# Near attention's first two batches moved into the last product of the values, with the PSUM banks turned round, three bias loads in one place and products of ones around a norm

## What is computed

```python
s_loc = jnp.einsum('bhrqd,bhrikd->bhrqik', qg, kg) * scale + bias      # bias gathered from rpb
s_loc = jnp.where(col_mask[:, None, :], s_loc, NEG_INF)
s_ctx = jnp.einsum('bhrqd,bhcd->bhrqc', qg, k_c) * scale
p = jax.nn.softmax(jnp.concatenate([s_loc, s_ctx], axis=-1), axis=-1)
o = einsum(p_loc, vg) + einsum(p_ctx, v_c)
x = x + g1 * (merge(o) @ odd_w_o)
x = x + g2 * conv_ffn(modulate(x, norm2_g, sh2, sc2), ...)
```

## Time and profile before

| what | us |
|---|---|
| median of 3 runs | 1559.91 (1559.86 to 1560.09) |
| the profiled execution | 1558.57 |
| its span, first to last instruction | 1556.8 |
| PE busy | 1529.9 (98%) |
| DVE busy | 1035.4 (67%) |
| ACT busy | 758.2 (49%) |
| POOL busy | 100.6 (6%) |

### The profile page before, as it was taken

One profiled execution on the slowest core, in us unless ns is written; L12 is line 12 of the kernel. 1 busy time (PEld: TensorE's weight loads), 2 busy tenths in 40 slices (PEclk: granted clock), 3 DMA queues, 4 the chain that ended last, 5 costly groups with the idle time before them and its releaser, 6 DMA issues.

```text
span 1556.8 us, 31388 instructions
## 1 busy us (share of the span) xinstructions
PE 1529.9 (98%) x13577; PEld 1464.8 (94%) x13577; DVE 1035.4 (67%) x1347; ACT 758.2 (49%) x1133; POOL 100.6 (6%) x79
## 2 busy tenths in 40 slices
PE   7999999999999999999999999999999999989999
PEld 7998999999999999999999999999999996889999
DVE  6777767578887775763567668876355348667675
ACT  5555555455455545653365322333255328655453
POOL 1311000003110000000020000000011003000000
PEclk9999999999999999999999999999999999999999
DMA  8776454576765545622045657663335224245864
GB/s 291 233 243 224 156 179 147 189 233 215 241 218 178 172 163 190 213 83 77 6 131 174 202 183 247 215 209 104 90 128 171 84 82 107 83 142 153 235 177 135
DMA packets 312637, 260.92 MB, mean 168 GB/s; under 512 B 24114, under 2 KB 298546, under 8 KB 312372
## 3 DMA queue, kind: packets, MB, share of 16 engines
q1 hardware_dynamic: 294884, 254.07, 50.4%
q10 hardware_dynamic: 17616, 4.85, 1.5%
HBM read 257.85 MB, written 1.05 MB: 166 GB/s over the span
## 4 chain that ended last, share of the span: by engine, by line
PE 57%; issue 7%; DVE 4%; ACT 2%; POOL 1%; DMA 0%; ACTq 0%; DVEq 0%; POOLq 0%
PE banks_g L1485 34%; PE banks_g L1011 8%; PE banks_g L1183 5%; DVE w_lo L2592 1%; ACT w_hi L1876 1%; PE banks_g L1347 1%; PE banks_g L1363 1%; PE banks_g L1000 1%; PE banks_g L1446 0%; PE bank_s L1519 0%; POOL bias L2204 0%; PE bank_t L1533 0%; PE bank_t L934 0%; PE bank_o L1158 0%; PE banks_g L991 0%
## 5 line engine op out<-in xcount | busy, mean ns | idle before, releaser
L1485 PE MATMUL banks_g<-h_hi,w_lo 128*128 128x256 f32 x1296 | 360.4, 278 | 1.5 <-DVE w_lo L2592 0.6
L1485 PE MATMUL banks_g<-h_lo,w_hi 128*128 128x256 f32 x1296 | 358.3, 277 | 0.0
L1485 PE MATMUL banks_g<-h_hi,w_hi 128*128 128x256 f32 x1296 | 358.3, 276 | 0.0
L2592 DVE TENSOR_TENSOR w_lo<-raw,w_hi 128x2048 fp32r<-128x2048 f32 (+1 forms) x100 | 208.0, 2083 | 97.7 <-ACT w_hi L1876 97.5
L2280 DVE TENSOR_TENSOR w_lo<-raw,w_hi 128x2048 fp32r<-128x2048 f32 x92 | 211.7, 2303 | 67.3 <-ACT w_hi L1662 66.7
L1485 PEld LDWEIGHTS banks_g<-h_hi,w_lo 128*128 128x128 f32 x1296 | 243.5, 188 | 3.7 <-issue 0.9
L1485 PEld LDWEIGHTS banks_g<-h_lo,w_hi 128*128 128x128 f32 x1296 | 243.4, 188 | 0.1
L1485 PEld LDWEIGHTS banks_g<-h_hi,w_hi 128*128 128x128 f32 x1296 | 243.4, 188 | 0.0
L1011 PE MATMUL banks_g<-h_hi,w_lo 128*128 128x256 f32 x800 | 225.9, 282 | 0.0
L1011 PE MATMUL banks_g<-h_lo,w_hi 128*128 128x256 f32 x800 | 221.4, 277 | 0.0
L1011 PE MATMUL banks_g<-h_hi,w_hi 128*128 128x256 f32 x800 | 221.4, 277 | 0.0
(11 more groups left out here) (433 smaller groups left out, 3256.4 us busy)
## 6 DMA issues: line engine op xcount, KB each, us to landing
raw<-w_in SPq DMA_DIRECT2D x75, 1024.0 KB, 4.8
raw<-w_up SPq DMA_DIRECT2D x88, 512.0 KB, 5.0
ada_raw<-ada_w SPq DMA_DIRECT2D x24, 1024.0 KB, 7.2
raw<-w_down SPq DMA_DIRECT2D x32, 704.0 KB, 4.5
raw<-w_branch SPq DMA_DIRECT2D x12, 1024.0 KB, 4.9
ada_raw<-ada_t SPq DMA_DIRECT2D x12, 1024.0 KB, 5.0
late_raw<-ada_t SPq DMA_DIRECT2D x12, 1024.0 KB, 5.0
raw<-qkv SPq DMA_DIRECT2D x12, 1024.0 KB, 5.0
```

Of the source, the lines that this page charges most:

```text
L1485: last = nc.tensor.matmul(to, w[:, c, m0:m0 + P], a[:, c, s_ * SEQ:s_ * SEQ + SEQ], start=(m, s_, c, n) == (0, 0, 0, 0), stop=(m, s_, c, n ...
L2592: nc.vector.tensor_tensor(w_lo[:, u % SLOTS, 0:n], raw[:, u % SLOTS, 0:n], w_hi[:, u % SLOTS, 0:n].bitcast(F32), ALU.subtract).then_inc(dv ...
```

## The change

It does five things.

1. `near_scores(1)` moves from behind nv31 to the middle of it, after 12 of its 48 products, and the exponentials of batches 0 and 1 move on ACT ahead of the emptying of nv31. nv31 itself waits for the emptying of the job two before it.
2. So that batch 1 has banks of its own, the order in which the jobs take the three banks is turned round from nv31 on (`end_bank`), odd batches score into banks 0 and 1, and odd batches' values go to bank 2.
3. The probabilities of batches 0 and 1 lie in other space (`near_first`), and so does the third bias tile (`bias_first`).
4. `load_bias(2)` moves from the first exponential to `qk squares q 0`: six bias DMAs stand there on ACT's list where four stood.
5. 9 products of ones (128x128 by 128 columns, f32, into a free bank) go ahead of `norm_sum` of the norm before `up1`, 3 ahead of its `norm_spread` and 10 behind it.

```diff
+        near_first = [sb(f"near_first{n}", [P, 2, 512], offset=f_hi_at + 4096 * n) for n in range(2)]
+        bias_first = sb("bias_first", [P, 4, SEQ], offset=f_lo_at + 4096)
...
+        def end_bank(k):
+            last = END_JOBS[("nv", 3, 1)]
+            return bank_g[k % BANKS if k < last else (last + BANKS - 1 - k) % BANKS]
+        def near_probs(b):
+            return near_first[b] if b < 2 else near_p[b % 3]
+        def near_bias(n):
+            return bias_first if n == 2 else bias[n % 3]
         def near_banks(b):
-            return bank_s[:, :, :].rearrange("p (e a) k -> p e (a k)", e=2) if b % 2 == 0 else banks_g[:, 1:3, :]
+            return bank_s[:, :, :].rearrange("p (e a) k -> p e (a k)", e=2) if b % 2 == 0 else banks_g[:, 0:2, :]
...
+            def warm_up(n):
+                for _ in range(n):
+                    nc.tensor.matmul(spare_bank[:, 0:P], ones[:, :], ones[:, :], start=True, stop=True)
             def norm_sum(tag, s_):
+                if tag == "11":
+                    warm_up(9)
...
             def norm_spread(tag, s_):
+                if tag == "11":
+                    warm_up(3)
...
+                if tag == "11":
+                    warm_up(10)
...
                             if (i, j) == (3, 1):
+                                pe.wait_ge(act_steps, act_.at(f"empty{k - 2}"))
                                 near_scores(0)
                             for tt in range(2):
                                 for c in range(KC):
+                                    if (i, j, tt, c) == (3, 1, 0, 4):
+                                        near_scores(1)
...
+                        if (kind, i, j) == ("nv", 3, 1):
+                            near_exp(0)
+                            near_exp(1)
                         act.wait_ge(pe_steps, pe_.at(f"job{k}"))
...
-                        for n in range(2):
+                        for n in range(3):
                             load_bias(n)
...
                 elif what == "near exp":
                     b, = arg
-                    if b == 0:
-                        act.wait_ge(pe_steps, pe_.at(f"job{END_JOBS[('nv', 3, 1)]}"))
-                        load_bias(2)
+                    if b < 2:
+                        continue
```

More of the change, by code:

```diff
@@ L1192, in near_scores @@
                 if b == 1:
-                    pe.wait_ge(act_steps, act_.at(f"empty{END_JOBS[('nv', 3, 1)]}"))
+                    pe.wait_ge(act_steps, act_.at(f"empty{END_JOBS[('nv', 3, 0)]}"))
                 if b >= 2:
@@ L1233, in up_first @@
                 ks = [END_JOBS[("up0", i, j)] for i, j in ((0, 0), (0, 1), (1, 0))]
-                to = [bank_g[k % BANKS] for k in ks]
+                to = [end_bank(k) for k in ks]
                 pe.wait_ge(dve_steps, dve_.at(f"lo{u0}"))
@@ L1263, in up_second @@
                 for c in range(KC):
-                    last = products(bank_g[k0 % BANKS][:, SEQ:2 * SEQ], wh, wl, h2_hi, h2_lo, c, 0, 1, KC)
+                    last = products(end_bank(k0)[:, SEQ:2 * SEQ], wh, wl, h2_hi, h2_lo, c, 0, 1, KC)
                 last.then_inc(pe_steps, pe_.step(f"job{k0}"))
@@ L1571, in _ @@
                 elif what == "near scores":
-                    if arg[0]:
+                    if arg[0] >= 2:
                         near_scores(*arg)
@@ L1591, in _ @@
                         pe.wait_ge(dve_steps, dve_.at(f"near o{b - 2}"))
-                    ob = bank_o if b % 2 == 0 else bank_g[0]
+                    ob = bank_o if b % 2 == 0 else bank_g[2]
                     for kt in range(4):
@@ L1901, in hidden_high, with near_exp @@
                                      ).then_inc(act_steps, act_.step(f"f hi{ly} {i}"))
+            def near_exp(b):
+                act.wait_ge(dve_steps, dve_.at(f"near max{b}"))
+                if b >= 3:
+                    act.wait_ge(pe_steps, pe_.at(f"near turn{b - 3} 1"))
+                for e in range(2):
+                    nc.scalar.activation(near_probs(b)[:, e, :], near_banks(b)[:, e, :], ACT.Exp,
+                                         bias=near_max[:, b % 2, e:e + 1], accum_out=near_sum[:, b % 2, e:e + 1]
+                                         ).then_inc(act_steps, act_.step(f"near exp{b}"))
             for what, *arg in END:
@@ L2105, in _ @@
                     b, = arg
-                    if b == 0:
-                        act.wait_ge(pe_steps, pe_.at(f"job{END_JOBS[('nv', 3, 1)]}"))
-                        load_bias(2)
-                    if b >= 2 and b % 2 == 0 and b // 2 + 2 < 8:
+                    if b < 2:
+                        continue
+                    if b % 2 == 0 and b // 2 + 2 < 8:
                         act.wait_ge(dve_steps, dve_.at(f"near masked{b - 1}"))
                         load_bias(b // 2 + 2)
[L2114 to L2121, removed]
+                    near_exp(b)
                 elif what == "near turn":
@@ L2599, in multiply @@
                 job = END_JOBS[(f"up{ly}", i, 1 if ly == 0 else 0)]
-                vb = spare_bank if (ly, i) == (0, 1) else bank_g[job % BANKS][:, 0:512] if ly == 0 else bank_g[job % BANKS][:, SEQ:2 * SEQ]
+                vb = spare_bank if (ly, i) == (0, 1) else end_bank(job)[:, 0:512] if ly == 0 else end_bank(job)[:, SEQ:2 * SEQ]
                 dve.wait_ge(act_steps, act_.at(f"silu{ly} {i}"))
```

32 lines of the change are left out of this document (16 added, 16 removed).

## The result

The changed kernel takes 1567.62 us (median of 5 runs, 1566.38 to 1569.02); the kernel before took 1560.09 in the same comparison (5 runs, 1559.86 to 1562.88). The ratio is 1.0042 with a 95% interval of 1.0031 to 1.0053: slower by 7.5 us by the medians, by 6.6 us by the ratio. The profiled execution after the change is the one of 1569.02 us, with a span of 1566.1.

The account below looks back on a forecast made before the run. PE, busy 98% of the span, was taken as the bound, so only its waits and clock count. +6.7 and +1.9, -2.2 and -0.8 give +5.6 us on 1558.57, then 1.34 to the median: 1565.5 us, range 1561.5 to 1568.0.

Parts of the forecast that it names:

- the mechanism that was named: Bias issues into a full queue hold ACT, PE waits at nk 1's second job, and that idle time costs clock.
- the forecast's own bounds: Whole kernel: issue and clock losses less gains give +3.7 to +6.7 us, 1563.6 to 1566.6.
- rival (c): Near attention or norm: gains don't come, 1 to 3 us less gained, 1566.5 to 1568.5; chance 0.13.
- The bias loads: ACT ahead of the queries' squares: six issues start the squares 6.7 us later, delaying PE at nk 1's second job.
- Rival (a): Bias loads on ACT: issues are cheap, at most 1.4 us for two more; 1558.3 or 1556.9 us; chance 0.15.
- The step's model: ACT's DMA queue: takes a DMA in 0.69 us while it has room, then only as transfers drain; holds about 2,600 packets.
- The clock: PE around nk 1's second job: idle time lowers the granted clock, costing 1.9 us, bounds 0 and 3.4.
- Rival (b): Bias loads: queue blocks but drains faster, 4.5 us, shorter idle costs 0.9 us of clock; 1562.3 us; chance 0.12.
- Near attention: First batches: PE's three waits on ACT, 2.32 us, go; a second break in nv31 costs 0.1; gain 2.2 us.
- The norm: Norm before up1: products of ones hold the clock, so its first unit ends 0.8 us sooner, bounds 0 and 0.9.
- the sign: Norm before up1: PEclk 1.00 throughout, first unit ending 0.7 to 0.9 us sooner after the last wo product.
- Behind the norm PE has one wait of 0.6 us left: After the norm before up1: with only that PE wait left, gains or losses ahead of it reach the end.

Follow-up runs that it names:

- long rows: Changed kernel with the third bias tile's two DMAs at q 0 replaced by two of 4 KB rows, the real load at k 1: 1563.89 us, 1.0018.
- ones in the stall: Changed kernel plus 32 products of ones on PE ahead of its wait at the second job of nk 1: 1566.22 us, 1.0034.
- six loads alone: Kernel before with only the bias loads changed: six DMAs ahead of the queries' squares, third tile in its own space: 1571.07 us, 1.0061.
- the pairs of runs: Three pairs of versions, each with and without the products of ones at the norm; with ones the median is lower by 0.4, 0.5 and 0.8 us.
- sixth of long rows: Changed kernel with five bias DMAs at q 0, then one of 80 packets; third tile's second real load at k 1: 1567.61 us, single run.
- one tile at a time: Changed kernel with two bias DMAs at each of the squares of q 0, k 0 and k 1: 1556.88 us, 0.9974.

## Why the prediction was right

The forecast was 1565.5 us, and 1567.62 was measured, inside the range and slower, by the mechanism that was named. It lies near the upper end of that range, though, and 1.0 us above the forecast's own bounds (1563.6 to 1566.6); the room came from rival (c). Step by step:

- **The bias loads** (forecast +6.7 us, and PE's wait 6 to 7.5 us): +7.19, the wait 7.70, a little over that. Moving the two issues away takes the whole loss out, and adding them to the kernel before brings it there. Rival (a), cheap issues, falls with the fifth and sixth at 2.89 and 4.44 us. The size is 0.5 us short because the last issue ended later than the forecast had it: when 3,857 packets of the bias DMAs had begun (4,289 less 432) and not 3,680, so that 2,383 were left and not 2,600. In the profiled execution 3,680 had begun 0.4 us before that. The step's model came close to the total and was wrong in one part: it gave a DMA's own packets a share, and the runs with long rows showed that what stands ahead holds the issue.
- **The clock** (forecast +1.9): +2.29, shown by ones in the stall, which bring it to 0. The price does not follow the length of the wait: 1.59 us of loss for a wait of 2.54, 2.27 for 4.20, 2.29 for 7.70, 2.12 for 8.01 (six loads alone). Rival (b)'s idea that a shorter stall costs half the clock was therefore too kind: the wait of 4.20 us cost 2.27, not 0.9. By the Trainium skill's rule of length times missing share (TensorE: Matmul & The Clock Gate, Terms), the two stretches of 4 us at 0.50 alone would cost an estimated 4.0 us. The rows show 2.29, as PE waits through the first and the start of the second anyway.
- **Near attention** (forecast -2.2): the offset between the two timelines falls from 11.40 us at the root to 9.10 at scores 3 (1299.38 against 1290.28), so -2.30. Of that 0.30 is lost again by the first product of `wo`. The prediction read no wait from batch 4 on; the kernel before has one of 0.19 us ahead of scores 9, and the changed kernel one of 0.49 ahead of scores 10, both on the exponentials. Their difference is the 0.30:

```profile
1310.49 1.13 PE L1199 MATMUL banks_g<-k_n,q_n 64*128 64x512 f32 x4 [0.19 <-ACT near_p L2119]
...
1323.22 1.13 PE L1214 MATMUL bank_s<-k_n,q_n 64*128 64x512 f32 x4 [0.49 <-ACT near_p L1940]
```

- **The norm** (forecast -0.8): -0.51 at the end of its first unit, short of the 0.7 to 0.9 us that were named as the sign. The clock held, as forecast; the second chunk still finds PE waiting 0.72 us, and the chunks, not PE, set the pace. The three products ahead of the spread cost about 0.1 us: DVE had written `token_rstd` by 1374.42, and the spread began at 1374.57. Then the step "Behind the norm PE has one wait of 0.6 us left, so what is gained or lost ahead of it reaches the end" failed in this execution: it read where PE waits, and not how little it is ahead elsewhere. In the kernel before, the low part of a `down1` weight ended at 1528.52, 0.17 us before PE used it:

```profile
1526.90 1.62 DVE L2592 TENSOR_TENSOR w_lo<-raw,w_hi 128x1408 fp32r<-128x1408 f32 x1 [0.85 <-ACT w_hi L1876]
...
1528.69 0.28 PE L1485 MATMUL banks_g<-f_hi,w_lo 128*128 128x256 f32 x1
```

  After the change PE comes sooner against that split, and waits:

```profile
1536.25 1.62 DVE L2626 TENSOR_TENSOR w_lo<-raw,w_hi 128x1408 fp32r<-128x1408 f32 x1 [0.85 <-ACT w_hi L1906]
...
1537.93 0.38 PE L1515 MATMUL banks_g<-f_hi,w_lo 128*128 128x256 f32 x1 [0.18 <-DVE w_lo L2626]
```

  The stretch behind the first unit is 0.47 us longer, and all of it is lost here: PE runs 8.89 us later than in the kernel before up to this job, and 9.36 us later from there on. With the gain of 0.51 that leaves nothing in this execution. The other profiled executions agree that the gain shrinks, not where: from the first unit's end to the last transposes the four without ones take 178.05 to 178.17 us and the eight with ones 178.34 to 179.69, or 181.62 in the one whose products ran slower (last section); three of the eight show no wait for a weight's low part. So less was gained than forecast, as in rival (c) but not for its reasons, by about 0.8 us and not by 1 to 3; the pairs of runs leave open whether 0.4 to 0.8 us of it reach the median.

So the forecast's sum of +5.6 came out 1.9 us under the measured +7.5. All four terms erred in the same direction: 0.5 from the issues, 0.4 from the clock, 0.2 from near attention, and 0.8 from the ones.

## What to carry to other kernels

A DMA issue is not free for the engine that makes it: read the lengths of successive issues in its timeline. Where they rose here, from the third of six on, each issue paid for those ahead. Put loads of many short rows a few at a time into gaps of the engine's list, ahead of work that has slack; here the last two of six DMAs cost 7.37 us in one place, and two in each of three places cost 0.6 to 0.7 us each. A gain on a busy engine can be lost again where it meets work that was only just in time, so look for small margins as well as for waits.

## What was not expected of the hardware

An issue's length hung on the packets ahead of it: an issue of 80 packets took 3.15 us as the fifth and 5.57 as the sixth behind bias loads, but 0.62 behind another of 80.

The loss of clock came almost whole with a short wait: 1.59 us for 2.54 us of waiting, and 2.27 for 4.20 in the run with long rows, against 2.29 for 7.70 and 2.06 for 8.64 (sixth of long rows, a single run).

Products also run at two paces while the granted clock reads 1.00. Two stretches of the same length of the execution profiled for one tile at a time, in both of which PE is busy throughout:

```profile
1400.00:1420.00 20.00, 20.00 (x179) 20.00 (x178) 13.55 (x19) 11.39 (x14) 0.00 (x0) 1.00 0.62 180
1480.00:1500.00 20.00, 20.00 (x173) 20.00 (x172) 13.59 (x17) 11.02 (x13) 0.00 (x0) 1.00 0.65 192
```

The kernel before has 179 products in the later stretch too. From the first `up1` unit's end to the last transposes this execution takes 181.62 us where the kernel before takes 178.05, and its time is 3.7 us above its version's median. The two paces may be part of what spreads the runs of one kernel; that isn't shown, and why they happen is open.
